# Norms, gates and running sums made beside the input projection of a stick-breaking / HGRN2 / mixture-of-experts trunk

## The chip, the cores and the metric

The kernel runs on one core of a Trainium2 chip. The metric is the device time of one execution in microseconds. A core has five engines that run beside one another and meet at semaphores: TensorE (PE in the profile, its weight loads PEld), VectorE (DVE), ScalarE (ACT), GpSimd (POOL) and SyncE (SP, which here only issues DMAs). TensorE's clock has two levels, 1.2 and 2.4 GHz; the profile gives the granted clock as a share of full speed, so 0.50 is the lower level throughout.

## The reference, cut to what matters

One layer, 1024 tokens of width 1024. The input is normed and multiplied by `w_in` (1024 x 3584), which gives the attention's q, k and v (8 heads of 64 each) and the recurrence's q, f, i and gate (4 heads of 128 each).

```python
q = rms_norm(heads(sb_q), sb_q_norm_g[l]); k = rms_norm(heads(sb_k), sb_k_norm_g[l])
a = stick_breaking_attention(q, k, heads(sb_v))      # strictly causal, blocks of 128 queries
# recurrence, in blocks of 32 tokens, for each head:
log_f = log(lb + (1 - lb) * sigmoid(f));  kf = (1 - lb) * sigmoid(-f)
b = cumsum(log_f)                        # inside the block of 32
q_e = q * exp(b);  k_e = kf * exp(-b)
o = ((q_e @ k_e.T) * causal) @ v + q_e @ state
state = exp(b_last)[:, None] * state + (kf * exp(b_last - b)).T @ v
```

`lb`, the lower bound, comes from a softmax over two rows of logits. Then `x = x + concat(headnorm(a), headnorm(r) * silu(gate)) @ w_out`, and a mixture of 32 experts, four for each token, whose weights (384 MB) are streamed. Only `q_e @ state` and the state's own line need the state; norms, gates, `b`, `q_e` and `k_e` need nothing but the projection.

## The kernel before, in words

The program is a series of blocks. Inside a block each engine has its own instruction list, ordered by semaphore waits written by hand; between blocks all engines meet. The blocks in order are: first norm and transposes; input projection (L238); query and key norms (L317); attention (L450); recurrence (L605); mixing norms and output gate (L838); output projection, second norm and router; the expert loop.

**Input projection.** `w_in` is taken in 14 chunks of 256 columns. SP loads a chunk, ScalarE casts it to fp16 (high part, L250), GpSimd subtracts to get the low part (L257), and TensorE multiplies the parts in three products (high x high, high x low, low x high). A chunk has four pieces, one for each of banks 0 to 3. "Major" chunks (L272) come out channel-major, channels on partitions and 512 tokens in a bank, into `cm` (region_b). The others (L281), which are v, f and i, come out token-major into `tm` (region_c). VectorE copies every piece out (L295, L297). Each engine loops with `Fori` over pairs of chunks. A piece may be overwritten when the same piece of the chunk before it has been copied out.

**Query and key norms.** For each of 8 channel tiles: ScalarE squares it (L333), TensorE sums over a head with a matrix of ones in f32 (L361), ScalarE makes the inverse root with Ln and Exp (L339, L342), VectorE multiplies (L394), and GpSimd and VectorE split the result in an fp16 high and low part (L421, L401) in region_a, `qk16`. VectorE also makes the lower bound, from logits loaded at the start of this block and spread over all partitions (L369 to L380).

**Attention** (48 steps, written out): TensorE's scores (L539), masks (L544), exponents (L553, L558) and values (L569), VectorE's caps and maxima (L476, L485), ScalarE's exponentials (L513 to L520).

**Recurrence.** Eight tiles of 128 tokens, each with four blocks of 32. For a later tile VectorE caps f (L699), ScalarE makes the sigmoid with Exp, Ln, Exp (L642, L649, L651), GpSimd does the affine part of the gate (L619, L621), VectorE the key (L704, L706), and ScalarE Ln (L655). TensorE makes the running sum with a triangular matrix of ones (L764) and transposes the keys (L769). ScalarE takes exp(b) and exp(-b) (L661, L663), VectorE makes q_e, k_e and the decayed keys (L712, L714, L717). TensorE transposes these (L775), computes scores (L779), masked by VectorE (L722), the state updates (`updates`, L790: 16 matmuls, each over the 32 partitions of one block, block outside and head inside), the block's own output (L798), and the output from the states (`out_states`, L808: 16 matmuls with 32 moving columns). VectorE folds the updates into the state (`states`, L733: 16 steps in a chain of four blocks). The updates of the next tile overwrite the banks that `states` reads.

**Mixing.** SP loads `w_out` in one 4 MB DMA; GpSimd casts and splits it in eight steps (L851, L853). Beside that ScalarE, TensorE and VectorE norm the eight channel tiles (L871, L917, L941, L946), and the last four get the output gate (L928, L932, L939).

## Time and profile before

| | us |
|---|---|
| median of 3 runs | 2348.84 (2348.03 to 2352.6) |
| profiled execution | 2342.38 |
| its span | 2340.6 |
| PE busy | 2168.0 (93%) |
| PEld busy | 1860.7 (79%) |
| DVE busy | 1566.5 (67%) |
| ACT busy | 1417.5 (61%) |
| POOL busy | 636.7 (27%) |

The span is what the trace covers; the profiled execution is its device time, 1.8 us longer, and it is 6.5 us under the median of the unprofiled runs. A busy share is a mean over stages with different limits: the expert loop, from about 880 us on, weighs most in it. The change touches only what lies ahead of 790 us, so the stages there have to be read one by one.

### The profile page before, as it was taken

How to read it: one execution, taken by the hardware profiler on the slowest of the kernel's cores; microseconds unless marked ns; L12 is line 12 of the kernel's file. 1: busy time of each engine (PE TensorE's matmuls, PEld its weight loads, DVE VectorE, ACT ScalarE, POOL GpSimd, SP SyncE). 2: the span in 40 equal slices, each digit the busy share in tenths (PEclk: the TensorE clock that was granted, in tenths of full speed). 3: DMA queues.
4: the chain of work that ended last, by engine and by line, in shares of the span. 5: the costliest groups of instructions: out<-in, count | busy, mean ns of one | idle time of the engine just before them, and what ended most of it. 6: DMA issues, size and time to landing. Idle time of an engine off the chain costs nothing.

```text
span 2340.6 us, 60909 instructions
## 1 busy us (share of the span) xinstructions
PE 2168.0 (93%) x24825; PEld 1860.7 (79%) x24825; DVE 1566.5 (67%) x1958; ACT 1417.5 (61%) x1659; POOL 636.7 (27%) x409
## 2 busy tenths in 40 slices
PE   5999987998894695999999999999999999999998
PEld 3476833433791354999999999999999999999997
DVE  3111126444776314788888888888888888888886
ACT  4000026555326424687787787787777787787784
POOL 1221113332315012332332322422422422422321
PEclk8999998999775796999999999999999999999999
DMA  4111100000003116798898898898898889889887
GB/s 153 54 45 46 36 10 0 1 1 1 1 1 143 39 81 236 266 331 310 324 328 307 319 333 307 319 328 311 317 326 319 318 313 329 314 311 336 311 309 238
DMA packets 141679, 489.83 MB, mean 209 GB/s; under 512 B 11658, under 2 KB 26762, under 8 KB 141568
## 3 DMA queue, kind: packets, MB, share of 16 engines
q1 hardware_dynamic: 128768, 445.30, 51.6%
q0 software_dynamic: 12864, 43.88, 7.8%
q8 instruction: 33, 0.54, 0.1%
q14 instruction: 14, 0.11, 0.0%
HBM read 457.86 MB, written 35.52 MB: 211 GB/s over the span
## 4 chain that ended last, share of the span: by engine, by line
PE 55%; DVE 3%; DMA 2%; issue 1%; ACT 0%; POOL 0%; POOLq 0%; DVEq 0%; SPq 0%; ACTq 0%
PE banks L1654 50%; PE banks L1648 2%; DVE region_c L1486 2%; PE banks L1634 1%; DMA rows_out<-region_b 1%; PE banks L1621 1%; DMA region_b<-rows_out,region_d 0%; DMA region_d<-w_down_dram 0%; DVE region_b L1512 0%; DMA rows_out<-region_b,region_d 0%; ACT region_b L1341 0%; ACT region_b L1327 0%; POOL region_b L1251 0%; DVE region_b L1501 0%; DVE region_b L1593 0%
## 5 line engine op out<-in xcount | busy, mean ns | idle before, releaser
L1654 PE MATMUL banks<-region_b,region_c 128*128 128x160 f16 x18432 | 1299.9, 233 | 5.7 <-DVE region_b L1512 1.8
L1654 PEld LDWEIGHTS banks<-region_b,region_c 128*128 128x128 f16 x18432 | 1281.3, 98 | 9.4 <-DVE region_c L1486 4.3
L1486 DVE TENSOR_TENSOR region_c<-region_a,region_c 128x4096 f16<-128x4096 f32 x128 | 565.3, 4416 | 25.6 <-ACT region_c L1321 17.3
L1321 ACT ACTIVATE region_c<-region_a 128x4096 f16<-128x4096 f32 x128 | 462.5, 3613 | 44.2 <-DMA region_a<-w_gate_up_dram 40.9
L1255 POOL DMA_INDIRECT region_b<-rows_h,region_d x64 | 294.6, 4602 | 35.8 <-issue 28.5
L1321 ACT ACTIVATE region_c<-region_d 128x4096 f16<-128x4096 f32 x64 | 231.5, 3618 | 96.5 <-DMA region_d<-w_gate_up_dram 63.3
L1486 DVE TENSOR_TENSOR region_c<-region_d,region_c 128x4096 f16<-128x4096 f32 x64 | 282.5, 4414 | 2.7 <-ACT region_c L1321 2.7
L1264 POOL TENSOR_TENSOR region_d<-region_d 80x1 f32<-80x1 f32 x96 | 19.6, 204 | 922.3 <-DVE region_d L1463 656.7
L272 PE MATMUL banks<-region_a,region_d 128*128 128x512 f16 x768 | 167.8, 381 | 8.1 <-POOL region_d L257 8.1
L250 ACT ACTIVATE region_d<-region_d 128x2048 f16<-128x2048 f32 x14 | 26.6, 1909 | 234.6 <-PE banks L272 119.0
L1350 ACT ACTIVATE region_b<-banks,region_d 80x512 f32<-80x512 f32 x128 | 80.5, 678 | 135.2 <-PE banks L1648 126.7
L272 PEld LDWEIGHTS banks<-region_a,region_d 128*128 128x128 f16 x768 | 75.5, 98 | 99.6 <-issue 10.6
L281 PE MATMUL banks<-region_d,region_a 128*128 128x256 f16 x1152 | 126.1, 273 | 0.0
L295 DVE COPY region_b<-banks 128x512 f32 (+1 forms) x32 | 22.1, 692 | 152.9 <-PE banks L272 152.9
L281 PEld LDWEIGHTS banks<-region_d,region_a 128*128 128x128 f16 x1152 | 112.7, 98 | 13.5
L257 POOL TENSOR_TENSOR region_d<-region_d 128x2048 f16<-128x2048 f32 x14 | 56.9, 4065 | 236.6 <-ACT region_d L250 236.6
L1259 POOL DMA_INDIRECT rows_out<-region_b,region_d x66 | 99.6, 1509 | 41.7 <-issue 23.0
L476 DVE TENSOR_SCALAR region_d<-banks 128x1024 f32<-128x1024 f32 (+3 forms) x48 | 46.0, 958 | 94.5 <-PE banks L544 63.8
L1358 ACT ACTIVATE region_b<-banks,b_dcur 128x160 f32<-128x160 f32 x256 | 80.2, 407 | 28.8 <-PE banks L1654 28.8
L1337 ACT ACTIVATE region_b<-banks,region_d 128x160 f32<-128x160 f32 x256 | 85.3, 385 | 15.8 <-PE banks L1654 15.8
L1046 PE MATMUL banks<-region_c,region_a 128*128 128x512 f16 x256 | 80.2, 386 | 11.2 <-DVEq L1023 10.2
L297 DVE COPY region_c<-banks 128x512 f32 (+1 forms) x24 | 16.6, 691 | 109.0 <-PE banks L281 109.0
(257 smaller groups left out, 2398.9 us busy)
## 6 DMA issues: line engine op xcount, KB each, us to landing
region_a<-w_gate_up_dram SPq DMA_DIRECT2D x192, 1024.0 KB
region_d<-w_gate_up_dram SPq DMA_DIRECT2D x64, 1024.0 KB
region_a<-w_down_dram SPq DMA_DIRECT2D x64, 1024.0 KB
region_d<-w_down_dram SPq DMA_DIRECT2D x64, 1024.0 KB
region_d<-w_in_dram SPq DMA_DIRECT2D x14, 1024.0 KB, 5.0
region_b<-x_dram SPq DMA_DIRECT2D x8, 1024.0 KB, 8.8
region_c<-w_out_dram SPq DMA_DIRECT2D x1, 4096.0 KB, 12.8
rows_out<-region_b SPq DMA_DIRECT2D x8, 512.0 KB, 2.6
```

The lines of the kernel that those rows point to most:

```text
L257: pool.tensor_tensor(w_par[par][:, 1], w_raw[par], w_par[par][:, 0], ALU.subtract).then_inc(s_wlo, 1)
L272: mm = pe.matmul(bank[q][:, :], a, b, start=(k == 0 and j == 0), stop=(k == KT - 1 and j == 2))
L281: mm = pe.matmul(bank[q][:, tt * WC:(tt + 1) * WC], a, b, start=(k == 0 and j == 0), stop=(k == KT - 1 and j == 2))
L1046: mm = pe.matmul(bank[half][:, :], a, b, start=(k == 0 and j == 0), stop=(k == KT - 1 and j == 2))
L1255: pool.indirect_dma_start(out=xg[:, h, :], out_offset=None, in_=rows_h2[:, :], in_offset=bass.IndirectOffsetOnAxis(ap=rows_get[:, h:h + 1] ...
L1259: pool.indirect_dma_start(out=rows_out[:, :], out_offset=bass.IndirectOffsetOnAxis(ap=rows_prev[:, h:h + 1], axis=0), in_=yrow[:, h, :], i ...
L1321: act.activation(part_hi[r], raw[r], ACT.Copy).then_inc(s_hi9, 1)
L1337: act.activation(u_all[:, f * SL:f * SL + SL], tile_at(3, f), ACT.Identity, bias=b_cur[:, KT + f:KT + f + 1]).then_inc(s_uev, 1)
L1350: act.activation(yrow[:, h, q * 512:q * 512 + 512], bank[Y_BANK[g]][0:HS, :], ACT.Copy, scale=gate_prev[:, h:h + 1]).then_inc(s_yrow, 1)
L1358: ins = act.activation(yT[:, f, :], tile_at(0, f), ACT.Identity, bias=b_dcur[:, f:f + 1])
L1486: dve.tensor_tensor(part_lo[r], raw[r], part_hi[r], ALU.subtract).then_inc(s_lod, 1)
L1654: mm = pe.matmul(out_ap, a, b, start=(first and s == 0), stop=(k == KT - 1 and s == 2), skip_group_check=True)
```

## The change

The block for the norms is gone, and the recurrence's block has lost all that does not need the state. Both are done in the block of the input projection, chunk by chunk.

- All loops of the projection are written out. The order of the chunks is now: q and k of the attention (0 to 3), f (4, 5), q of the recurrence (6, 7), v (8, 9), i (10, 11), output gate (12, 13). f comes out channel-major, into `f_cm`.
- Norms: during chunk m = 1 to 4 the two channel tiles of chunk m-1 are squared (ScalarE), summed (TensorE, four f32 matmuls of 512 columns between pieces 1 and 2, in banks 4 to 7), normed and split. The fp16 parts, `cm16`, lie over the tiles of `cm` that they come from.
- Gates: during chunk 8 + h head h is capped, goes through the sigmoid, its gate (the affine part is in ScalarE's scale and bias) and key; the running sum is one VectorE `tensor_tensor_scan` over 1024 tokens, with a row of resets that is 0 at the start of each block of 32. q_e and k_e are made in place, and the last exp(b) of each block is kept in `eb_last`.
- The lower bound is made for 4 columns, from logits loaded at the very start.
- The recurrence keeps `scaled_keys`, the transposes and their copy, scores, mask, `updates`, `states` and the two outputs. `updates` has heads outside and blocks inside. GpSimd has no part in it, and i is read from `tm` without a copy.
- Attention writes its output to `a_cm` in region_d and its scratch lies in region_a. In the mixing block `w_out` comes in eight 512 KB DMAs through a ring of four.

```diff
+        CHUNKS = ([(n * WC, cm, 2 * n) for n in range(4)] + [(2048 + n * WC, f_cm, 2 * n) for n in range(2)] +
+                  [(1536 + n * WC, cm, 8 + 2 * n) for n in range(2)] + [(1024 + n * WC, None, n * WC) for n in range(2)] +
+                  [(2560 + n * WC, None, 512 + n * WC) for n in range(2)] + [(3072 + n * WC, cm, 12 + 2 * n) for n in range(2)])
...
+                def decays(h):                                   # ScalarE
+                    act.wait_ge(s_fc, h + 1)
+                    act.activation(t_e, t_e, ACT.Exp, scale=-1.0).then_inc(s_ef, 1)
...
+                    act.activation(t_r, t_e, ACT.Ln, bias=ones[:, 0:1]).then_inc(s_rf, 1)
...
+                    act.activation(t_r, t_r, ACT.Exp, scale=-1.0).then_inc(s_rf, 1)
+                    act.wait_ge(s_kf, h + 1)
+                    act.activation(t_r, t_r, ACT.Ln, scale=oml_col[:, h:h + 1], bias=lb_col[:, h:h + 1]).then_inc(s_lf, 1)
+                    act.wait_ge(s_b, h + 1)
+                    act.activation(t_r, f_cm[:, h, :], ACT.Exp).then_inc(s_ebr, 1)
...
+                    act.activation(t_n, f_cm[:, h, :], ACT.Exp, scale=-1.0).then_inc(s_ebr, 1)
...
+                for m in range(NC):                              # TensorE
+                    pe.wait_ge(s_wlo, m + 1)
                     for q in range(PC):
+                        piece(m, q)
+                        if q == 1 and 1 <= m < HT + 1:
+                            sums(2 * (m - 1))
+                            sums(2 * (m - 1) + 1)
...
+                def keys_and_sums(h):                            # VectorE
+                    dve.wait_ge(s_rf, 2 * h + 2)
+                    dve.scalar_tensor_tensor(out=t_e, in0=t_e, scalar=oml_col[:, h:h + 1], in1=t_r, op0=ALU.mult, op1=ALU.mult).then_inc(s_kf, 1)
+                    dve.wait_ge(s_lf, h + 1)
...
+                    dve.tensor_tensor_scan(out=f_cm[:, h, :], data0=resets, data1=t_r, initial=0.0, op0=ALU.mult, op1=ALU.add).then_inc(s_b, 1)
...
+                for m in range(NC):
+                    pair = (2 * (m - 1), 2 * (m - 1) + 1) if 1 <= m < HT + 1 else ()
+                    h = m - PRE_AT if PRE_AT <= m < PRE_AT + NH else None
+                    if h is not None:
+                        capped_f(h)
+                    evac(m, 0)
+                    if h is not None:
+                        keys_and_sums(h)
+                    evac(m, 1)
+                    for c in pair:
+                        normed(c)
+                    if h is not None:
+                        scaled(h)
+                    evac(m, 2)
+                    for c in pair:
+                        low(c)
+                    evac(m, 3)
...
+                def updates(t):                                  # recurrence, TensorE
+                    pe.wait_ge(s_kdtm, t + 1)
+                    if t > 0:
+                        pe.wait_ge(s_st, t * SPT)
+                    for h in range(NH):
+                        for c in range(NB):
+                            rows = slice(c * RB, (c + 1) * RB)
+                            mm = pe.matmul(u_bank[c][:, h * P:(h + 1) * P], kd_tm[t % 2][rows, h * P:(h + 1) * P],
+                                           tm[rows, t, SBW + h * P:SBW + (h + 1) * P], start=True, stop=True)
+                    mm.then_inc(s_u, 1)
...
+                inner(0)
+                for t in range(NT):
+                    updates(t)
+                    if t + 1 < NT:
+                        inner(t + 1)
+                    out_att(t)
+                    out_states(t)
```

## Rows read from the trace of the kernel before

**Rows 1.** Windows: us, busy per engine (instructions), granted clock, DMA share, GB/s.
```profile
338.00:376.00 38.00, 18.06 (x37) 6.74 (x38) 33.72 (x43) 29.18 (x51) 13.91 (x16) 0.81 0.00 0
569.00:706.00 137.00, 118.42 (x801) 105.24 (x800) 88.40 (x187) 43.06 (x69) 31.68 (x25) 0.79 0.00 0
```
**Rows 2.** The page's groups: matmuls and splits of the input projection's channel-major chunks.
```profile
L272 PE MATMUL banks<-region_a,region_d 128*128 128x512 f16 x768 | 167.8, 381 | 8.1 <-POOL region_d L257 8.1
...
L257 POOL TENSOR_TENSOR region_d<-region_d 128x2048 f16<-128x2048 f32 x14 | 56.9, 4065 | 236.6 <-ACT region_d L250 236.6
```
**Rows 3.** A window of the first block, and the timeline (start, us) behind it.
```profile
22.00:24.00 2.00, 1.28 (x8) 1.05 (x7) 1.60 (x2) 1.94 (x5) 0.00 (x0) 1.00 0.00 0
...
33.80 3.71 ACT L250 ACTIVATE region_d<-region_d 128x2048 f16<-128x2048 f32 x2 [1.27 <-PEq L261]
```
**Rows 4.** Timeline: the projection's last copy, attention's first matmuls; window there.
```profile
333.25 0.69 DVE L295 COPY region_b<-banks 128x512 f32<-128x512 f32 x1 [4.49 <-PE banks L272]
...
375.82 0.50 PE L539 MATMUL banks<-region_a 64*128 64x128 f16 x6 [8.77 <-PEq L317]
...
375.00:380.00 5.00, 4.18 (x28) 2.15 (x28) 2.77 (x5) 3.56 (x5) 0.40 (x1) 0.50 0.00 0
```
**Rows 5.** Timeline of TensorE in attention: pairs of f32 matmuls, 512 columns.
```profile
560.13 1.98 PE L553 MATMUL banks<-region_d,neg_tri 128*128 128x512 f32 x4
561.95 1.88 PE L558 MATMUL banks<-region_b,neg_ones 128*128 128x512 f32 x4
```
**Rows 6.** Timeline of ScalarE in attention: 1024 columns.
```profile
560.30 1.15 ACT L520 ACTIVATE region_d<-region_d,ones 128x1024 f32<-128x1024 f32 x1
```
**Rows 7.** Timeline of VectorE in the recurrence: beside GpSimd, then without it.
```profile
674.99 1.76 DVE L704 TENSOR_TENSOR region_d<-region_d 128x512 f32<-128x512 f32 x1
...
686.68 0.69 DVE L717 TENSOR_TENSOR region_d<-region_d 128x512 f32<-128x512 f32 x1
687.79 4.60 DVE L733 SCALAR_TENSOR_TENSOR region_a<-region_a,region_d,banks 128x128 f32<-128x128 f32 x16 [0.42 <-PE banks L790]
```
**Rows 8.** Timeline: ScalarE's first and last instruction of the recurrence.
```profile
581.90 1.28 ACT L636 ACT_TABLE_LOAD   x1 [2.16 <-PEq L450]
...
706.20 0.60 ACT L680 ACTIVATE region_b<-banks 128x512 f32<-128x512 f32 x1 [11.90 <-PE banks L808]
```
**Rows 9.** Timeline of TensorE in the recurrence, at either clock.
```profile
597.27 1.12 PE L775 MATMUL banks<-ident,region_d 128*128 128x128 f32 x4 [4.40 <-DVE region_d L717]
598.18 1.91 PE L779 MATMUL banks<-region_d 128*128 128x128 f32 x8
...
602.59 2.96 PE L790 MATMUL banks<-region_d 32*128 32x128 f32 x32
605.48 1.16 PE L798 MATMUL banks<-region_a,region_d 128*128 128x128 f32 x8
...
606.91 1.06 PE L779 MATMUL banks<-region_d 128*128 128x128 f32 x8
...
615.51 5.13 PE L790 MATMUL banks<-region_d,region_a 32*128 32x128 f32 x32
...
690.01 3.66 PE L808 MATMUL banks<-region_d,region_a 128*128 128x32 f32 x32
...
699.29 6.87 PE L808 MATMUL banks<-region_d,region_a 128*128 128x32 f32 x32
```
**Rows 10.** Timeline of TensorE in attention: scores, two row groups in turn.
```profile
396.39 0.82 PE L539 MATMUL banks<-region_a 64*128 64x512 f16 x6
```
**Rows 11.** Windows: the clock behind the state outputs that began at 690.
```profile
694.00:695.00 1.00, 1.00 (x16) 1.00 (x16) 0.00 (x0) 0.30 (x1) 0.00 (x0) 1.00 0.06 16
695.00:699.00 4.00, 4.00 (x26) 3.77 (x23) 1.43 (x6) 0.00 (x0) 0.00 (x0) 0.51 0.00 0
```
**Rows 12.** Windows: mixing, beside GpSimd's casts and after them.
```profile
720.00:751.00 31.00, 11.83 (x15) 3.74 (x14) 29.26 (x16) 17.81 (x30) 30.11 (x16) 0.61 0.35 135
751.00:786.00 35.00, 8.83 (x10) 2.35 (x8) 21.39 (x35) 25.68 (x42) 0.00 (x0) 0.50 0.00 0
```

607 lines of the change are left out of this document (250 added, 357 removed).

## The prediction

> **What bounds the kernel now.** I read the page's table of slices first, then the trace in windows by stage, then the timelines of TensorE, VectorE and ScalarE around each stage boundary. Some 1,460 us of the 2,340.6 us span are the expert loop, where PE is busy at a granted clock near full; the change leaves it alone. What it touches is the 450 us between about 334 and 786 us. The query/key norms take a stage of their own, 338 to 376, in which PE is busy 18.1 of 38 us and ScalarE and VectorE hand tiles to one another; the recurrence takes 569 to 706 with PE busy 118 of 137 us, at a mean granted clock of only 0.79 [rows 1]. The projection ahead of both is PE's: its eight channel-major chunks take 167.8 us, 21.0 each, and the six others do the same work. Beside such a chunk GpSimd has one instruction of 4.1 us [rows 2], ScalarE one of 1.9 us [rows 3], and VectorE four copies of 0.7 us. So there is room there on three engines, and none on PE.
>
> **Step 1, the norms move into the projection.** The last projection copy ends at 333.9 and attention's first matmul starts at 375.8 [rows 4]: 41.9 us, of which about 0.3 is the crossing of a block, which stays. All the rest of the stage goes, the lower-bound arithmetic (it becomes 4 columns wide) included. What comes back is PE work, because PE is the projection's bound: 16 f32 matmuls of 512 columns. In attention two of that size take 1.98 us, and the next pair starts 1.82 us behind [rows 5], so 16 cost 8 x 1.82 = 14.6 us. I charge them in full: four go between pieces 1 and 2 of chunks 1 to 4. Upper bound, if no pair overlapped its neighbours: 8 x 1.98 = 16; a lower one would need a faster clock than full. Net 41.6 - 14.6 = 27 us gained.
>
> Does the rest hide? In chunks 1 to 4 ScalarE does high (1.9), four squares, and four Ln/Exp pairs at about 0.65 each: under 11 us of 24.6. The squares that PE's sums wait for are done about 5 us into the chunk, and PE asks for them after two pieces, 10.5 us in. GpSimd does 4.1 us and then two casts. The next chunk's weights are split (1.9 + 4.1 us) 15 us before they are needed, and the weight DMA waits for the same split as before. The two new small loads stand ahead of the first weight load on SP's queue, but ScalarE starts on that one at 33.8 us, while DMA is idle from 22 us on [rows 3]: nothing. Writing the loops out costs nothing unless instruction fetch shows; attention is already written out so and shows no such wait.
>
> **Step 2, gates and sums move beside chunks 8 to 11.** One head per chunk: ScalarE has six 1024-column instructions at up to 1.15 us [rows 6], VectorE a cap, three products and the scan. In line: 1.9 (weight split) + 0.8 (cap) + 6 x 1.15 + 1.4 + 1.3 + 1.3 (products) = 13.6 us and the scan. No row shows a scan. From the nearest, a 512-column f32 product at 0.69 us, 1.76 us where GpSimd works [rows 7], it is between 1.4 us and twice the slow rate, 7 us; I take 2.5. So 16 us of 21.0, and PE waits only for copies of the chunk before: cost 0, with 5 us of slack per head. PE does none of this work.
>
> **Step 3, the recurrence keeps only what needs the state.** It now runs from 581.9 (its table load) to 706.8 (its last copy) [rows 8], 124.9 us: 20.7 us until the first state update at 602.6 [rows 9], and 103.6 us for eight tiles, 12.95 each. After: ahead of the first update stand a memset 0.5, scaled keys 0.7, transposes 1.1, a copy 0.6 and their hand-overs, 4.5 us in all. Per tile PE has four things [rows 9]. At the full clock: updates 2.9, values and transposes together 1.43 (start to start), scores 0.9 without the overlap, state outputs 3.6. At half clock: updates 5.1, transposes 0.9, scores 1.8, values 1.9 (about twice 1.0), state outputs 6.9. The running sums and the key transposes of each tile are gone.
>
> The updates also change order: heads outside, row groups inside, so that neighbours use different 32-row groups and different banks. No row has four such groups; attention's scores alternate two, and six 512-column fp16 matmuls take 0.82 us [rows 10] where six full-rate ones (218 ns each by rows 2) would be 1.31, a ratio of 0.63. For four groups I take 0.5; the bounds are 1 (the weight loads may set the pace) and 0.25. The Trainium skill, "TensorE: Matmul & The Clock Gate", Part 3, gives 3.07x for four row tiles of 512 columns; by that the updates would be 0.94 us, an estimate by that page, and the whole 4 us less.
>
> So a tile costs PE 1.45 + 1.43 + 0.9 + 3.6 = 7.4 us at the full clock and 2.5 + 0.9 + 1.8 + 1.9 + 6.9 = 14.0 at half. VectorE's own cycle is shorter: 16 state steps in 4.60 us, starting when the updates end, plus 0.7 mask and 0.7 keys [rows 7]; updates plus states are 6.2 us. GpSimd leaves this stage, so the slow products (1.76 for 0.69) do too. So PE and its clock decide. The rows say how that clock behaves: after 3.7 us of state outputs (32 moving columns each) at the full clock, it fell to half at 695 with PE busy in every record of the stretch [rows 11]. The state outputs were about a quarter of a tile and become half, so I expect a larger share of the time at half clock than the 0.79 mean stands for (40% of the time): 60%. Then a tile takes 1/(0.4/7.4 + 0.6/14.0) = 10.3 us, eight take 82, less 2 for the last, which has no next tile: 80. With 4.5 and 0.7 for the last copy: 85. Gain 40 us.
>
> **Step 4, the rest.** Attention now starts behind a working PE instead of one that waited 8.8 us: it began at half clock [rows 4], and of 5 us so spent I take 2 as gained (0 to 4), as PE does not set the pace of these first steps alone. In the mix stage w_out comes in eight pieces, so GpSimd starts sooner. That does not shorten the stage: while GpSimd casts, VectorE's 16 instructions of a 31 us window fill 29.3 us, and right after 35 instructions take 21.4 [rows 12]. The slow stretch is as long and only lies earlier. 0 us, give or take 4. Here the Trainium skill, "GPSIMD Engine Reference", 8. Key points, says that GpSimd shares its SBUF interfaces with VectorE for instructions with two SBUF inputs, and the trace agrees (1.76 against 0.69). That rule speaks against this change, since norms and gates are put beside GpSimd's weight split: by it the moved products would be 2.5 times as long for 4 us of each 21, some 4 us more per chunk, still inside the slack.
>
> **Sum.** 27 + 40 + 2 = 69 us. The profiled execution took 2342.4 (span 2340.6): it would become 2273. The runs' median is 2348.8, 6.5 above it, so the predicted time is 2280.
>
> **Rivals.**
> A, the forecast: chance 0.55; own range 2265 to 2298.
> B, state outputs keep the clock at half nearly all through. For: at 699 to 706 the last tile ran so, 6.87 us for its outputs [rows 9]. Against: with the old mix it recovered each time within 10 us. Then the stage is 5.2 + 8 x 14.0 - 2 = 115, gain 10: 27 + 10 + 2 = 39, 2310. Chance 0.22.
> C, the clock stays full. For: PE has fewer waits than now. The stage is 5.2 + 8 x 7.4 - 1 = 63, gain 62: 27 + 62 + 2 = 91, 2258. Chance 0.18. The Trainium skill, "TensorE: Matmul & The Clock Gate", Why this matters for your kernels, asks only that there be no PE idle gaps between bursts; that would make C likely. The row at 695 speaks against it, as the clock fell without a gap.
> D, the moved work becomes the projection's bound and the kernel is slower. The place is chunks 8 to 11, where one head's chain of ScalarE and VectorE has to fit a chunk; from a chain of 21.0 us on, each microsecond costs four. To eat 69 us it would have to be 21 + 17 = 38 us, against my 16; if every VectorE term ran at the contended rate all through, it would be 27 and cost 26. Time where it decides, 2352. Chance 0.03.
> E, the change does not do what it says in one part: the new order gives no overlap of row groups, so the updates stay at 2.9 and 5.1. It costs 8 x 2 = 16 us over A: 2296, inside A's range and part of A's chance. That the move as a whole gives nothing (2348, were PE to stall in the written-out projection by all that it saves) has 0.02.
>
> **How the numbers follow.** C with full overlap of the row groups is 2252, B without it 2330. I leave out a tenth at each end: 2256 to 2312. A measurement of this kernel tells 0.2% (4.7 us) from nothing. Faster by more: A, B, C = 0.95. Within: 0.02 (E). Slower: 0.03 (D).
>
> **What would show it.** The projection should last about 14.6 us longer, and attention's first matmul should come near 349 us. PE should show no wait for VectorE or GpSimd in chunks 8 to 11. The recurrence should last about 85 us, with a granted clock near 0.7, and the first update some 4 to 5 us in. The update group should take about half its old time per matmul. The mix stage should keep its length. I am wrong if the projection grows by over 25 us, if the state loop is paced by VectorE, or if its clock is above 0.9.

## The result: 101 us faster, 32 us beyond the forecast

| | before | after |
|---|---|---|
| median of the runs, us | 2349.14 | 2247.7 (2245.88 to 2252.61, 4 runs) |
| ratio, 95% interval | | 0.9569 [0.9551, 0.9587] |
| profiled execution, span | 2342.38, 2340.6 | 2252.61, 2250.7 |
| attention starts | 375.8 | 348.3 |
| recurrence starts | 581.9 | 551.7 |
| mixing starts | 707.1 | 613.4 |
| output projection starts | 786.1 | 691.6 |

A second run of the kernel after gave 2247.41 us (2245.96 to 2250.2). One execution of e2 (3715.53 us) and one of e5 (7447.3 us) were in a slow state and are left out. The forecast was 2280 with a range of 2256 to 2312, so the time lies below the range. The direction was right, and so were three of the four steps. The recurrence was forecast at 85 us and takes 61.7.

The stages are read from ScalarE's table loads, one at the start of each. The columns are start, duration, engine, line, and in brackets the idle time before it. Kernel after, recurrence and mixing, and then output projection:

```profile
551.73 1.28 ACT L633 ACT_TABLE_LOAD   x1 [2.16 <-PEq L487]
...
613.40 1.28 ACT L789 ACT_TABLE_LOAD   x1 [0.27 <-PEq L630]
...
691.61 1.28 ACT L924 ACT_TABLE_LOAD   x1 [1.15 <-PEq L758]
```

The differences of the table's columns give 27.5 us up to attention, then attention 2.7 shorter (206.1 to 203.4), recurrence 63.5 (125.2 to 61.7), mixing 0.8, and 4.6 us lost behind it, in stretches that the change doesn't touch: 89.9 in the profiled executions.

### The profile page after: what moved, and what is told of

It is laid out like the page before. It is cut to its first block, busy times and chain, and to the rows that moved or that the text cites. A ratio compares the mean times of both kernels' runs of the same rounds, so it can differ in the third digit from the quotient of the medians.

```text
span 2250.7 us, 59693 instructions
## 1 busy us (share of the span) xinstructions
PE 2116.3 (94%) x24537; PEld 1796.4 (80%) x24537; DVE 1548.6 (69%) x1933; ACT 1412.7 (63%) x1633; POOL 604.2 (27%) x379
## 4 chain that ended last, share of the span: by engine, by line
PE 57%; DVE 3%; DMA 2%; issue 1%; ACT 1%; POOL 0%; POOLq 0%; DVEq 0%; SPq 0%; ACTq 0%
PE banks L1580 52%; PE banks L1574 3%; DVE region_c L1412 2%; PE banks L1560 1%; DMA rows_out<-region_b 1%; PE banks L1547 1%; DMA region_d<-w_down_dram 0%; DMA region_b<-rows_out,region_d 0%; ACT region_b L1267 0%; DMA rows_out<-region_b,region_d 0%; DVE region_b L1438 0%; ACT region_b L1253 0%; ACT region_b L1263 0%; POOL rows_out L1185 0%; POOL region_b L1177 0%
## 5 line engine op out<-in xcount | busy, mean ns | idle before, releaser
L345 PE MATMUL banks<-region_a,region_d 128*128 128x512 f16 x960 | 210.9, 382 | 7.8 <-POOL region_d L319 7.8
L345 PEld LDWEIGHTS banks<-region_a,region_d 128*128 128x128 f16 x960 | 94.6, 99 | 124.3 <-POOL region_d L319 8.2
L319 POOL TENSOR_TENSOR region_d<-region_d 128x2048 f16<-128x2048 f32 x14 | 57.0, 4074 | 201.3 <-ACT region_d L265 201.3
L400 DVE COPY region_b<-banks 128x512 f32<-128x512 f32 x32 | 22.1, 692 | 127.9 <-PE banks L345 127.9
L513 DVE TENSOR_SCALAR region_a<-banks 128x1024 f32<-128x1024 f32 (+3 forms) x48 | 46.0, 958 | 91.4 <-PE banks L581 60.7
L550 ACT ACTIVATE region_a<-banks 128x1024 f32<-128x1024 f32 (+3 forms) x48 | 38.9, 810 | 77.9 <-PE banks L595 76.5
L353 PE MATMUL banks<-region_d,region_a 128*128 128x256 f16 x768 | 84.0, 273 | 0.0
L353 PEld LDWEIGHTS banks<-region_d,region_a 128*128 128x128 f16 x768 | 75.1, 98 | 8.9
```

The costliest lines, as they stand in the source:

```text
L345: mm = pe.matmul(bank[q][:, :], a, b, start=(k == 0 and j == 0), stop=(k == KT - 1 and j == 2))
L353: mm = pe.matmul(bank[q][:, tt * WC:(tt + 1) * WC], a, b, start=(k == 0 and j == 0), stop=(k == KT - 1 and j == 2))
```

## The profile after

**The projection.** The page's groups of the kernel after, answering to [rows 2] (ten chunks are channel-major now, eight were before), and the group of the moved norm sums:

```profile
L345 PE MATMUL banks<-region_a,region_d 128*128 128x512 f16 x960 | 210.9, 382 | 7.8 <-POOL region_d L319 7.8
...
L319 POOL TENSOR_TENSOR region_d<-region_d 128x2048 f16<-128x2048 f32 x14 | 57.0, 4074 | 201.3 <-ACT region_d L265 201.3
...
L362 PE MATMUL banks<-region_d,head_ones 128*128 128x512 f32 x32 | 14.4, 592 | 0.0
```

A matmul takes 382 ns where it took 381, and the only idle time in front of this group is the first wait for GpSimd, as before. GpSimd's split is no slower either, 4,074 ns for 4,065. So the moved work costs PE nothing beyond its own matmuls, 3.44 us start to start in each of four chunks. The timeline at the boundary answers to [rows 4]: first VectorE's last copy, then PE.

```profile
347.31 0.69 DVE L400 COPY region_b<-banks 128x512 f32<-128x512 f32 x1 [4.49 <-PE banks L345]
```
```profile
345.81 1.46 PE L345 MATMUL banks<-region_a,region_d 128*128 128x512 f16 x6
348.32 0.34 PE L576 MATMUL banks<-region_b 64*128 64x128 f16 x6 [1.05 <-PEq L252]
```

PE stands still for 1.05 us between projection and attention, where a stage of 38 us stood. One head's gates, on VectorE beside chunk 8:

```profile
222.64 0.68 DVE L422 TENSOR_SCALAR region_b<-region_c 128x1024 f32<-128x1024 f32 x1
...
227.88 1.37 DVE L426 SCALAR_TENSOR_TENSOR region_b<-region_b,oml_col 128x1024 f32<-128x1024 f32 x1
230.55 2.29 DVE L430 TENSOR_TENSOR_SCAN region_c<-region_b 128x1024 f32<-128x1024 f32 x1 [1.31 <-ACT region_b L293]
...
235.21 1.22 DVE L438 TENSOR_TENSOR region_c<-region_b 128x1024 f32<-128x1024 f32 x1
```

ScalarE's weight split began at 222.1 and the last product ends at 236.4, so a head takes 14.3 us of a chunk of 21. GpSimd's split in this chunk runs from 224.1 to 228.2, and the scan and the products of 1.22 us come after it. So the forecast's allowance of 4 us a chunk, for products slowed beside GpSimd, was not needed, and this order doesn't put it to the test.

**The recurrence.** Windows answering to [rows 1], whose columns they share: the whole stage, four microseconds with the start of a fall of the clock at their end, the fall itself, and the rest of the loop.

```profile
551.70:613.10 61.40, 59.51 (x672) 57.70 (x672) 46.06 (x145) 10.80 (x17) 0.00 (x0) 0.93 0.01 1
574.00:578.00 4.00, 4.00 (x59) 3.96 (x58) 2.95 (x9) 0.60 (x1) 0.00 (x0) 0.96 0.00 0
578.00:582.00 4.00, 4.00 (x30) 3.78 (x26) 3.45 (x13) 0.60 (x1) 0.00 (x0) 0.62 0.00 0
582.00:612.00 30.00, 30.00 (x356) 29.36 (x354) 22.96 (x75) 4.18 (x7) 0.00 (x0) 1.00 0.01 2
```

In 57.5 us of loop (555 to 612.5) PE is never idle, and the clock is 0.95. It stands at half in the first tile, once from about 578 to 581, and as the stage ends. One tile at full clock, answering to [rows 9]:

```profile
562.98 1.17 PE L711 MATMUL banks<-region_c,region_d 32*128 32x128 f32 x32
564.08 0.66 PE L695 MATMUL banks<-ident,region_d 128*128 128x128 f32 x4
564.57 1.06 PE L700 MATMUL banks<-region_b,region_c 128*128 128x128 f32 x8
565.47 1.06 PE L720 MATMUL banks<-region_d,region_c 128*128 128x128 f32 x8
566.36 3.66 PE L732 MATMUL banks<-region_b,region_d 128*128 128x32 f32 x32
569.95 1.17 PE L711 MATMUL banks<-region_c,region_d 32*128 32x128 f32 x32
```

From update to update it is 6.97 us. The updates take 1.10 us start to start where they took 2.9: the four row groups do overlap, with a ratio of 0.38.

## The experiments

### What holds the clock up: the repeat, and the parts of a tile

**e13, the kernel after unchanged**, to see whether its clock is its own.

> The kernel after, unchanged, over five rounds beside the kernel with w_out made early. Recurrence 60 to 64 us at a clock of 0.92 to 0.96, mixing 78 us, median 2246 to 2251 us. If the clock of the recurrence is a matter of where each execution stands, and not of the kernel alone, single executions reach 2255 to 2265 us and the profiled recurrence may come out at 65 to 75 us.

Measured: recurrence 61.9 us, loop clock 0.95, mixing 78.3, median 2247.41. The high clock belongs to the kernel and isn't luck of one execution. Six profiles hold this recurrence with its outputs in one row (the kernel after, e13, e6, e7, e8, e12): the stage took 60.2 to 68.0 us, and every one of them has at least one fall of the clock in the loop behind its first tile.

**e1, the updates in the old order.**

```diff
-                    for h in range(NH):
-                        for c in range(NB):
-                            rows = slice(c * RB, (c + 1) * RB)
+                    for c in range(NB):
+                        rows = slice(c * RB, (c + 1) * RB)
+                        for h in range(NH):
```

> The changed kernel, with the state updates issued as before the change: row group (block) outside, head inside. Three theories of why TensorE's clock stayed near full in the state loop (0.95 from 555 to 612 us), where the prediction had it at half for 60% of the time. S, the share: the clock follows the share of time that goes to the state outputs (32 moving columns); here that share falls a little, so the clock stays at 0.95 or above and only the updates get longer, 2.9 for 1.10 us a tile: state stage 61.4 + 8 x 1.8 = 76 us, the whole +14. W, the waits: the clock falls where PE waits for VectorE ahead of the state outputs; there is no such wait in either order, so the same 76 us. R, the row groups: four updates side by side keep the array busier and hold the clock; undone, the clock goes back to about 0.8 and the stage takes 85 to 95 us.

Measured: median 2289.23 (2277.46 to 2296.89), recurrence 107.7 us. The loop, 555 to 657.4:

```profile
555.00:657.40 102.40, 102.40 (x660) 100.19 (x658) 44.72 (x143) 8.36 (x14) 0.00 (x0) 0.63 0.00 1
```

Every theory said less. Serial updates (neighbours in the same row group, so that they don't overlap) cost 1.7 us more per tile at the full clock, 14 in all; the stage grew by 46. The other 32 came through the clock, which fell to 0.63 although PE was busy in all of 102.4 us. The profiled execution is the slowest of the four, though: by the medians the kernel lost 41.5 us, and its fastest execution 30. All are well above 14. So this swap of two loops is worth more than its own duration, and the forecast gave it only that.

**e2, the state outputs wait until the whole chain of states is done.**

```diff
+                    pe.wait_ge(s_st, (t + 1) * SPT)     # at the head of out_states
```

> The changed kernel, with the state outputs of a tile held until all 16 state steps of that tile are done; same results. PE then waits some 2 us a tile ahead of the outputs, and a tile is updates 1.1 + states 4.7 + outputs 3.6 = 9.5 us at the full clock in place of 7.0. S (the clock follows the share of state outputs, which falls from 0.52 to 0.38): clock 0.95 or more, stage 61.4 + 20 = 81 us. W (waits ahead of the outputs bring the clock down): mean granted clock 0.6 to 0.8 and a stage of 95 to 110 us.

Measured: executions of 2280.04, 2280.96 and 2284.86 us, recurrence 98.4 us, clock 0.70, PE idle for 14 us of the stage. The range of W held, not that of S.

**e3, 15 of 16 state outputs twice**, the second time into an unused bank.

```diff
+                            if c < NB - 1 or h < NH - 1:
+                                pe.matmul(bank[0][:, at:at + RB], here[c][:, h * P:(h + 1) * P],
+                                          cm[:, 2 * HT + h, t * P + c * RB:t * P + (c + 1) * RB], start=True, stop=True)
```

> The changed kernel, with 15 of the 16 state outputs of a tile done twice, the second time into a bank that nothing reads. PE has 3.4 us more a tile, no wait more, and the state outputs take 0.68 of its time. Without any change of the clock: 61.4 + 27 = 88 us for the stage, the whole +27. S (share): the clock goes to half for most of the stage, 110 to 140 us. W (waits): the clock stays at 0.9 or above, 88 to 93 us.

Measured: median 2303.95 (2299.76 to 2305.35), recurrence 114.7 us.

```profile
555.00:665.50 110.50, 110.50 (x902) 108.07 (x900) 45.01 (x143) 8.36 (x14) 0.00 (x0) 0.72 0.00 1
```

S was right here, with PE busy throughout: a wait isn't needed for the fall. Its clock falls with the updates in the new order too: the first fall begins at about 564 us, inside the doubled row of outputs, which started at 559.5. After e1 to e3 neither S nor W alone held: e1 was against both, e2 against S, e3 against W.

**e5, dense padding**: 8 products of 128 columns more in each tile, behind the updates.

```diff
+                def padding(t):
+                    for n in range(8):
+                        h = n % 4
+                        pe.matmul(bank[0][:, h * P:(h + 1) * P], f_cm[:, h, t * P:(t + 1) * P], cm[:, 2 * HT + h, t * P:(t + 1) * P],
+                                  start=True, stop=True)
```

> The changed kernel, with eight more f32 matmuls of a full 128 x 128 array and 128 moving columns a tile, right behind the state updates, into a bank that nothing reads: 1.8 us of PE a tile at the full clock, the same time that the old order of the updates adds. Order back made the stage 107.7 us for 61.7, at a clock of 0.63, where its own time is only 14 us. T, thin work: only work that uses a part of the array (row groups in series, 32-column outputs) or a wait brings the clock down; full matmuls of the same length don't: clock 0.93 or more, stage 61.7 + 14 = 76 us. L, length: any longer tile changes how the outputs fall against the clock's decisions, so the clock goes to 0.6 to 0.8 here too, 90 to 108 us.

Measured: executions of 2270.31, 2271.55 and 2273.11 us, recurrence 83.8 us, loop clock 0.86, so both ranges were missed. Two windows of the loop:

```profile
590.00:594.00 4.00, 4.00 (x39) 4.00 (x37) 1.42 (x3) 0.00 (x0) 0.00 (x0) 1.00 0.01 2
594.00:598.00 4.00, 4.00 (x44) 3.74 (x44) 1.80 (x7) 0.60 (x1) 0.00 (x0) 0.57 0.01 4
```

The outputs ran from 590.5 to 594.1, and the clock fell right behind them, and so in every tile from 570 us on (0.83 in each stretch of 10 us). More dense work in the tile made the falls regular instead of rare (one in the loop of the kernel after). That pointed at the row of outputs itself, and e10 and e11 put the question to it.

**e10, 12 products of 128 columns in place of 15 of the 16 outputs.**

```diff
                         for h in range(NH):
+                            if h < NH - 1:
+                                pe.matmul(bank[0][:, h * P:(h + 1) * P], here[c][:, h * P:(h + 1) * P],
+                                          cm[:, 2 * HT + h, t * P:(t + 1) * P], start=True, stop=True)
+                            if c < NB - 1 or h < NH - 1:
+                                continue
```

> The kernel after, with 15 of the 16 state outputs of each tile left out and 12 products of 128 columns into an unused bank in their place (their results are not used, so the output is not the reference's). Twelve at 0.265 us are 3.2 us of TensorE work for the 3.4 us left out: the engine stays as busy, only the shape of this work changes from 32 columns to 128. Theory C, the narrow outputs are what the clock falls behind: the recurrence's clock is 0.98 or more, no tile falls to the half level, and the recurrence is 57 to 60 us for 61.7. Rival B, the 32-row updates and their order are what counts, not the outputs: the clock stays where it was in the kernel after, 0.90 to 0.96, and the recurrence is 60 to 62 us. Rival P, what counts is where in the tile the work falls, whatever its shape, as the dense products of the padding kernel suggest, in which every tile fell to the half level behind the outputs: the clock may be anything down to 0.85, and the recurrence 60 to 68 us.

**e11, the same and the updates in the old order.**

> The same kernel (outputs replaced by wide products, output not the reference's) with the updates in the old order too, the block of rows outside and the head inside. In the run of that order with the real outputs the clock was 0.63 and the recurrence 107.7 us. The updates then take 2.85 us at the full level for 1.17. Theory C, the narrow outputs bring the clock down and the serial updates alone don't: clock 0.95 or more, tile 6.97 - 0.2 + 1.7 = 8.4 to 8.6 us, recurrence 71 to 76 us. Rival B, the serial updates alone bring it down: clock 0.75 or less, recurrence 90 to 105 us. Between 0.80 and 0.90 (78 to 88 us) it takes both.

Both kernels leave out 15 of the 16 outputs of each tile. Since the result differs, tokens are routed otherwise, and the expert loop has 19,008 matmuls for 18,432; so the medians (2281.41 and 2297.06) say nothing and only the stage is read. The loops of e10 and then of e11:

```profile
554.00:605.00 51.00, 50.57 (x616) 48.56 (x615) 45.00 (x143) 8.36 (x15) 0.00 (x0) 0.99 0.01 2
```
```profile
556.00:621.00 65.00, 64.78 (x602) 63.10 (x601) 43.02 (x139) 8.36 (x14) 0.00 (x0) 0.94 0.01 1
```

The stages were 55.2 and 71.4 us (e10 ran a little under the range expected, as its tile is 6.3 us and I had not reckoned that the narrow products left out took more than the wide ones put in). Theory C's reading held in both: with wide products in their place there is no fall in the loop. The serial updates, which with the real outputs went with a clock of 0.63, have 0.94 (C said 0.95 or more), and what is missing from 1.00 is only the first tile, which began at the lower level; from 564 us to the last product the clock is 1.00. Without waits of PE, the narrow outputs are the condition of the falls. How much the falls then cost depends on the updates beside them: with outputs narrow, 0.95 with the new order and 0.63 with the old.

**e14, the same instructions in another order**: the 16 outputs stand in three groups between dense products.

```diff
                 for t in range(NT):
                     updates(t)
-                    if t + 1 < NT:
-                        inner(t + 1)
                     out_att(t)
-                    out_states(t)
+                    out_states(t, (0,))
+                    if t + 1 < NT:
+                        turn_keys(t + 1)                # the transposes of inner
+                    out_states(t, (1,))
+                    if t + 1 < NT:
+                        scores(t + 1)                   # the scores of inner
+                    out_states(t, (2, 3))
```

> The kernel after with the same TensorE instructions in another order inside a tile: updates, products with the masked scores, the 4 outputs of the first block, the transposes of the next tile's keys, the 4 outputs of the second block, the next tile's scores, the 8 outputs of the last two blocks. The 16 narrow products no longer stand in one row of 3.4 us. Theory C (what the clock falls behind is an unbroken row of 32-column products): no tile falls to the half level, the loop's clock is 0.98 or more, the tile stays 6.97 us and the recurrence comes to 58 to 60 us for 61.7 to 61.9. Rival N (the share of narrow work in a tile counts, wherever it stands): clock 0.90 to 0.96 as before, 61 to 63 us. Rival Q (work that was safe in one piece now meets the narrow products more often, and the outputs of the second block wait for VectorE's steps): clock 0.70 to 0.88, 65 to 80 us.

Measured: recurrence 59.7 us, median 2247.18 (2243.51 to 2249.58). A tile, and the loop behind its first tile:

```profile
575.96 1.17 PE L713 MATMUL banks<-region_c,region_d 32*128 32x128 f32 x32
577.07 1.16 PE L722 MATMUL banks<-region_d,region_c 128*128 128x128 f32 x8
578.06 0.98 PE L734 MATMUL banks<-region_b,region_d 128*128 128x32 f32 x8
578.87 0.63 PE L695 MATMUL banks<-ident,region_d 128*128 128x128 f32 x4
579.34 0.98 PE L734 MATMUL banks<-region_b,region_d 128*128 128x32 f32 x8
580.15 1.14 PE L702 MATMUL banks<-region_b,region_c 128*128 128x128 f32 x8
581.13 1.87 PE L734 MATMUL banks<-region_b,region_d 128*128 128x32 f32 x16
```
```profile
557.00:610.00 53.00, 52.64 (x623) 51.40 (x622) 43.04 (x139) 8.68 (x15) 0.00 (x0) 1.00 0.01 2
```

The tile is still 6.97 us with the same work in it, and no fall is left behind the first tile. Against the 61.7 and 61.9 us of the kernel after this is 2 us, too little for the medians to show, and the duration alone would prove nothing: e6, with the same recurrence as the kernel after, took 60.2 us, as its first tile began at the full clock. What speaks for the order is the count of profiles with a fall behind the first tile: six of six with the outputs in one row, none of two with them spread (this one and e15).

### The projection: what is hidden and what is charged

**e6, the scan of each head six times** in place of once, 11.5 us more in one head's chain.

```diff
+                    for again in range(5):
+                        dve.tensor_tensor_scan(out=f_cm[:, h, :], data0=resets, data1=t_r, initial=0.0, op0=ALU.mult, op1=ALU.add).then_inc(s_again, 1)
+                        dve.wait_ge(s_again, 5 * h + again + 1)
```

> The changed kernel, with the running sum of each head made six times in place of once (same values). One scan takes 2.29 us, so the chain of a head in chunks 8 to 11, 14.3 us from the start of its chunk in the trace, becomes 25.8, longer than the chunk (20.5). The prediction's rival D: past the length of a chunk each microsecond costs PE one, so the projection grows by 4 x 5 = 20 us. Rival: PE is three pieces ahead of the copy that it needs, some 15 us, and the lateness grows over the four heads to 20, so that it pays only the last 5 us, or nothing but a start of chunk 12 that waits for the last head: 2 to 10 us.

Measured: attention starts 20.9 us later (369.14 for 348.28), and the median is 2269.61. PE's timeline has waits that the kernel after has nowhere, of 4.40, 5.90 and 4.86 us, one late in the work beside each of the last three heads. The first two, and windows behind the first wait, in the second, and behind the second:

```profile
272.83 22.53 PE L355 MATMUL banks<-region_d,region_a 128*128 128x256 f16 x192 [4.40 <-DVE region_c L404]
301.26 18.41 PE L355 MATMUL banks<-region_d,region_a 128*128 128x256 f16 x144 [5.90 <-DVE region_c L404]
```
```profile
272.80:277.00 4.20, 4.17 (x26) 3.20 (x27) 3.69 (x6) 3.23 (x3) 0.90 (x1) 0.65 0.00 0
295.40:301.20 5.80, 0.00 (x0) 0.00 (x0) 5.73 (x4) 0.55 (x1) 0.00 (x0) 0.86 0.00 0
301.20:306.00 4.80, 4.74 (x23) 3.37 (x24) 4.26 (x7) 3.26 (x3) 1.46 (x1) 0.50 0.00 0
```

The first head's chain of 14.3 us became 26.0. The prediction's rule for D, one microsecond for each of four heads from a chain of 21.0 us on, gives 4 x 5.0 = 20, and 20.9 came out. The sum agrees, but not by the rule's way. The waits are 15.2 us in all, and there is none beside the first head, where PE had work ahead of the copy it needs. Most of the other 5.7 us is the clock, which stood at 0.65, 0.50 and 0.53 in the four or five microseconds behind each wait. Nor was 26.0 the pace of the later heads: from one weight split to the next it is 28.4 us, since the next head's steps queue behind the copies. So the run shows that a chain longer than the chunk is paid for, and about how much; where the edge lies it doesn't measure. The change, at 14.3 us, stands 6 to 7 us below the length of a chunk.

**e8, the norm sums twice.**

```diff
-                        pe.matmul(bank[4 + 2 * (c % 2) + half][:, :], head_ones[:, :], sqrs[c % 2][:, half * 512:half * 512 + 512],
-                                  start=True, stop=True).then_inc(s_sumsq, 1)
+                        for again in range(2):
+                            mm = pe.matmul(bank[4 + 2 * (c % 2) + half][:, :], head_ones[:, :], sqrs[c % 2][:, half * 512:half * 512 + 512],
+                                           start=True, stop=True)
+                        mm.then_inc(s_sumsq, 1)
```

> The changed kernel, with each of the 16 f32 sums over a head done twice in the projection. The prediction charged the 16 in full to the end, at 14.6 us; the trace shows 3.44 us a chunk, 13.8. Twice: attention's first matmul moves from 348.3 to 362.1, the kernel is 14 us slower. Rival: the projection had room (waits of PE for pieces to be copied), and less than 10 us is added.

Measured: attention starts 13.6 us later (361.87), and the median is 2264.67 (2260.28 to 2266.72). The medians say 17.0. PE's work there is charged in full, as the forecast's 14.6 was.

### The kernel before, once with the new update order and once unchanged

**e4, the kernel before with `updates` in the new order** (the diff of e1 the other way round).

> The kernel before, with only the order of its state updates changed: heads outside, row groups inside. The updates go from 2.9 to about 1.15 us a tile at the full clock (5.1 to 2.3 at half). If PE's own time sets the pace there too: 14 to 18 us less in the recurrence. If VectorE's steps ahead of the states decide, as the wait of 1.07 us a tile ahead of the state outputs suggests, half of that, 5 to 9 us. R (row groups hold the clock): its mean rises from 0.80 to 0.9 or more and the gain is above 20 us.

Measured: median 2337.36 for 2350.47, ratio 0.9946 [0.993, 0.9963]; recurrence 117.3 us for 125.2. From one tile:

```profile
643.48 1.41 PE L790 MATMUL banks<-region_d,region_a 32*128 32x128 f32 x32
...
647.12 0.66 PE L775 MATMUL banks<-ident,region_d 128*128 128x128 f32 x4 [1.14 <-DVE region_d L717]
...
650.56 3.39 PE L808 MATMUL banks<-region_d,region_a 128*128 128x32 f32 x24 [1.07 <-DVE region_a L733]
```

The updates fell from 2.9 to some 1.3 us, but PE then waited for VectorE, for the decayed keys and for the state chain. Its clock in the loop (602.6 to 690) was 0.84, with PE idle for 13.8 of 87.4 us, so the theory R of 0.9 or more failed: the new order alone doesn't hold the clock up. By the profiles the order brings 8 us, by the medians 13.1; the first profile of the kernel before was a fast one (e9), so the 8 may be too few. Taken out of the kernel after, it costs 41.5 by the medians (e1): it pays in full only where the gates have left VectorE and PE is the bound.

**e9, the kernel before again**, for a second profile.

> The kernel before once more, unchanged, for a second profile of the same program. The profiled execution was 6 us faster than the median of the others, and the stages of the two profiles explain 95 us of the 101 us between the medians. If the recurrence's clock is what differs from one execution to the next, this one shows a stage of 125 to 140 us with a clock below or at 0.79 and every other stage the same to 1 us; if the expert loop is what differs, the recurrence is 124.9 us again and the stretch from mixing to the end (1633.5 us) is not.

Measured: 2352.27 us, recurrence 133.0 us, and from mixing to the end 1,633.6 us as in the first profile (1,633.5). What lies ahead of attention took 1.7 us longer, attention 0.2. Its loop:

```profile
604.00:716.00 112.00, 107.17 (x730) 102.40 (x728) 75.42 (x173) 28.86 (x52) 20.84 (x18) 0.72 0.00 1
```

The same instructions ran at 0.72 here and at 0.80 in the first profile. The kernel before varies by how often its clock falls, and the execution that the forecast was made from was a good one.

### A version that is faster still

**e7, `w_out` loaded, cast and split beside the recurrence**, where GpSimd and the DMA queues have nothing to do.

```diff
+        wo_raw = [region_a[:, n * D:(n + 1) * D] for n in range(KT)]
...
+            @block.sync                      # in the recurrence's block
+            def _(sp):
+                for k in range(KT):
+                    sp.dma_start(wo_raw[k], w_out[0, k * P:(k + 1) * P, :]).then_inc(s_wo[k], 16)
...
+            @block.gpsimd
+            def _(pool):
+                for k in range(KT):
+                    pool.wait_ge(s_wo[k], 16)
+                    pool.tensor_copy(wo_hi[:, k, :], wo_raw[k]).then_inc(s_wohi, 1)
+                    pool.wait_ge(s_wohi, k + 1)
+                    pool.tensor_tensor(wo_lo[:, k, :], wo_raw[k], wo_hi[:, k, :], ALU.subtract).then_inc(s_wolo, 1)
```

> The changed kernel, with w_out loaded, cast and split beside the recurrence, where GpSimd is idle, in place of beside the mixing norms (raw parts in region_a, high parts in the strips of region_c that held v, the recurrence's scratch in region_b). The mixing stage loses the 31 us in which GpSimd slows VectorE: 78 us becomes 64 to 68, so 10 to 14 us gained. Against it: in the recurrence the decayed keys (0.69 us, two SBUF inputs) take 1.7 us beside GpSimd, and are ready 1.0 us before PE asks for them. Theory T (thin work and waits lower the clock): if PE has to wait for them even a little, the clock falls and the stage grows from 61.7 to 75 us or more, which eats the gain. If only the waits themselves count: 2 us at most.

**e12, the same once more.**

> The kernel after with the loads, the casts and the low halves of w_out made beside the recurrence, a second time and over five rounds, to be set against the kernel after on the same chip. In the first run the recurrence was 62.2 us (after: 61.7) and the mixing 68.1 us (after: 78.2), and the profiled execution 14.6 us shorter; the medians differed by 4.5 only, with executions spread from 2236.6 to 2253.1. If the gain is that of the mixing, the median is 9 to 15 us below the kernel after's of this call. If the spread comes from this kernel (GpSimd beside the recurrence's VectorE steps lowers the recurrence's clock in some executions), its executions spread by 10 us or more again and the kernel after's do not, and the median is 2 to 8 us below.

**e15, the same with the outputs spread as in e14.**

> The same order of the outputs together with w_out's load, cast and low halves beside the recurrence. That kernel was profiled twice with the old order: recurrence 62.2 us at a clock of 0.94 and 67.9 us at 0.86, mixing 68.1 and 68.4 us. Theory C: recurrence 58 to 60 us in the profiled execution, mixing 68 us, median 2231 to 2236 us. Rival N: recurrence 62 to 68 us, median 2236 to 2243 us. Rival Q: above 2243 us.

| | median, executions | ratio to before | recurrence, loop clock | mixing |
|---|---|---|---|---|
| e7 | 2243.22 (2236.57 to 2253.05) | 0.9572 [0.9531, 0.9613] | 62.2, 0.94 | 68.1 |
| e12 | 2237.75 (2235.1 to 2246.36) | 0.9527 [0.9506, 0.9549] | 68.0, 0.86 | 68.3 |
| e13 (after) | 2247.41 (2245.96 to 2250.2) | 0.9572 [0.955, 0.9593] | 61.9, 0.95 | 78.3 |
| e15 | 2237.35 (2236.31 to 2238.01) | 0.9512 [0.9494, 0.953] | 59.8, 0.99 | 68.0 |

The loops of e12 and then of e15:

```profile
554.00:618.00 64.00, 63.34 (x664) 61.30 (x663) 48.21 (x143) 8.58 (x15) 26.19 (x16) 0.86 0.14 57
```
```profile
557.00:610.00 53.00, 53.00 (x628) 51.73 (x623) 43.18 (x139) 8.37 (x14) 25.89 (x16) 0.99 0.14 55
```

Mixing is 10 us shorter wherever GpSimd's 30 us of casts have gone, and beside the recurrence they lengthen VectorE's work by 3 us at most (49.2 for 46.1 in e12, 46.4 in e15), in the stage where it has room. e12 is 9.7 us below the kernel after measured beside it, as its first alternative said. Its executions spread by 11.3 us, as the second said, for 4.2 of the kernel after. Its profiled execution, 2246.36, was the slowest of its five, with the clock at half in three tiles. With the outputs spread, the five executions of e15 lie within 1.7 us, and its stage (59.8 us) is in theory C's range; its median, 2237.35, isn't, but in that of rival N. e15 is the fastest kernel of this study, 114 us below the kernel before (2351.28 beside it), but its median isn't below e12's by more than a measurement can tell. So the spread order is worth nothing in the medians; what it may bring is the steadiness, which one set of five executions suggests.

## Why the prediction was wrong

**Step 1, the norms: right.** Net 27 forecast, 27.5 measured, attention's first matmul at 348.3 where 349 was written. The sums were charged at 14.6 and take 3.44 us start to start in each of four chunks, 13.8.

**Step 2, the gates hidden: right, and tested.** The scan taken at 2.5 us is 2.29, the chain taken at 16 us is 14.3, and no wait of PE for it shows. e6 confirms that a chain past the length of the chunk is paid for; its agreement with D's price, 20.9 for 20, is in part luck, as 15.2 us were waits and most of the rest a slower clock behind them.

**Step 3, the recurrence: the step that failed.** At the full clock it said 7.4 us for a tile, and 6.97 was measured; the start-up said 4.5 and took 3.4. The failure is the sentence "I expect a larger share of the time at half clock than the 0.79 mean stands for (40% of the time): 60%". The clock in the loop was 0.95, some 10% of the time at half; the prediction had itself named a clock above 0.9 as a sign of being wrong. Its 80 us for eight tiles became 57.4 (555.1 to 612.5), and its own sum at the full clock, 8 x 7.4 - 1, gives 58. So nearly the whole miss is the clock. The step from 40% to 60% is only part of that: by the same formula, 40% gives 9.1 us a tile and a stage of 76 us. The sum carried a share over from the kernel before which the new mix of products didn't have.

The reasoning took the share of the narrow outputs in a tile as what decides: a quarter before, a half after. e10 shows that these outputs are indeed the condition. But e14 has the same share and no fall, and e1 has a smaller share and a clock of 0.63. What stands around the outputs decides as well: the serial updates (e1, 0.63), a wait of PE ahead of the outputs (e2, 0.70), more outputs in the row (e3, 0.72). The kernel before had serial updates and waits of PE together, at 0.80 and 0.72, and the change took both away. Taking away one of them isn't enough: e4, with the new order and the waits left, had 0.84, and e1, with no wait and the old order, 0.63.

The forecast hung on one fall, at 695 us [rows 11], behind outputs that ended at 693.6. The same trace has four more in the loop, at about 613.1, 640.5, 664.4 and 681.4 us. Two came within half a microsecond behind the row of outputs and two inside it, and no update stood there. Each of these four rows had a wait of PE of 0.9 to 1.1 us in it. The row of one of them, and windows around three:

```profile
661.85 0.98 PE L808 MATMUL banks<-region_d,region_a 128*128 128x32 f32 x8
663.89 4.94 PE L808 MATMUL banks<-region_d,region_a 128*128 128x32 f32 x24 [1.07 <-DVE region_a L733]
```
```profile
613.00:614.00 1.00, 1.00 (x7) 1.00 (x7) 1.00 (x3) 0.60 (x1) 0.61 (x1) 0.58 0.08 16
664.00:665.00 1.00, 1.00 (x7) 1.00 (x8) 1.00 (x4) 0.00 (x0) 0.00 (x0) 0.68 0.00 0
681.00:682.00 1.00, 1.00 (x8) 1.00 (x8) 1.00 (x5) 0.00 (x0) 0.00 (x0) 0.71 0.00 0
```

So the forecast named the right products. What it lacked was the other half. Two of the eight rows, at 624.2 and 651.4 us, had no fall; neither had a wait in it, nor had the one of 690, which did have a fall. That doesn't show that the waits were a cause, but it spoke for more than the share, and nothing in the trace said that twice the share would give more falls.

The prediction's window for the recurrence, 569 to 706 [rows 1], has the last 13 us of attention in it. Over the stage itself (581.9 to 707) the clock was 0.76, over its loop 0.80; the 40% fits the loop, so the slip cost nothing.

The smaller error beside it is the ratio of the updates, taken as 0.5 and measured as 0.38: 8 x 0.35 = 2.8 us.

**Step 4: right.** Attention gave 2.7 for 2, mixing 0.8 for 0.

**The rivals.** C, the clock stays full, was what happened. It had 2258, less 6.5 us for a profiled execution: 2251.5, and the profiled execution took 2252.6. By the medians it was 10 us high (2258 for 2247.7), and the range's low end, 2256, stood only 2 us under it. It had a chance of 0.18, as the rule of the Trainium skill behind it ("TensorE: Matmul & The Clock Gate", Why this matters for your kernels: no idle gaps between bursts) seemed refuted by the row at 695. The trace doesn't bear the rule out as the whole condition: in e1 the clock was 0.63 with PE busy in all of 102.4 us. PE's lack of gaps is what C and the kernel after have in common; it isn't enough by itself, and the order of the products has to come with it. That C's number came so near is in part two errors against each other: a tile 0.4 us shorter than it had, and the falls that it left out.

**From profile to median.** I added 6.5 us because the profiled execution was that far under the median. The profiled execution of the kernel after is 4.9 above its own. The medians differ by 101.4 us and the profiles by 89.8. e9 shows why the first profile of the kernel before was short: its recurrence takes 7.9 us longer than the first profile's, and all the rest together 2.0. The offset isn't a constant of the measurement but in the main the kernel's own variation in clock, so carrying it over was an error in itself. The 4.6 us behind the mixing are variation too, as far as the runs tell: that stretch takes 1,554.5, 1,554.7 and 1,557.0 us in the two profiles of the kernel before and in e4, 1,559.1 and 1,556.4 in two of the kernel after, and 1,554.1 in e7, whose code there is that of the kernel after.

**What stays open.** Why the clock falls behind some rows of outputs and not behind others: in the kernel after behind one of the eight rows and at the end of the last, with dense padding behind every one from 570 us on (e5). No run tells which property of the narrow products counts: their 32 columns or the length of their row. And whether e2's fall comes from PE's wait or from the outputs standing in one piece behind it.

## What to carry to other kernels

Work that needs only a chunk's own result can go beside the matmuls that make the next chunk; write down the chain per chunk and the chunk's length. Here a chain of 14.3 us in a chunk of 21 cost nothing, and one of 26 cost 20.9 us over four chunks, a part of it through the clock that fell behind PE's waits. Where the clock of a stage lies between its two levels, sum the stage at both, give each end its chance, and compare several executions before choosing a point between. If such a clock comes with rows of narrow products, try the same instructions in another order before counting instructions, and take the waits of TensorE away too.

## What was not expected of the hardware

- TensorE's clock fell to half with the engine busy in every record of a stretch: 0.63 over 102.4 us (e1), 0.72 over 110.5 us (e3). With 12 products of 128 columns in place of 15 of the 16 narrow ones it stayed at 0.99 (e10).
- Four row groups of 32 partitions, neighbours in different groups and banks, ran 16 f32 products of 128 columns in 1.10 us where the order by blocks takes 2.85: 2.6 times. The Trainium skill, "TensorE: Matmul & The Clock Gate", Part 3, has 3.07 for 512 columns; by it the updates would have been at 0.93 us, an estimate by that page. The trace has 1.10.
- GpSimd's casts beside the recurrence cost VectorE little: 46.1 us of work became 49.2 in e12, 48.1 in e7, 46.4 in e15. In e7 the 16 state steps of 128 columns, which take one input from a bank, needed 4.60 us beside GpSimd, as in the kernel before without it [rows 7]. A product of 512 columns with two SBUF inputs took 1.64 us there, and 1.76 for 0.69 in the kernel before [rows 7]. The two differ in width and in inputs; no run parts these.
- In e6 TensorE's clock stood at 0.65, 0.50 and 0.53 in windows of 4.2 to 4.8 us behind waits of 4.4 to 5.9 us.
